# Attention queue three deep instead of two, VectorE's weight split one step later, and the second mixer's output products begun inside its last attention steps

## The reference, cut to what matters

```python
# second mixer: 16 heads of 64+32 (scores) and 64 (values)
q = (rms_norm(cq, q_norm_g) @ w_q_b).reshape(B, S, MLA_HEADS, MLA_NOPE + MLA_ROPE)
kv = (rms_norm(ckv, kv_norm_g) @ w_kv_b).reshape(B, S, MLA_HEADS, MLA_NOPE + MLA_V)
...
s = (einsum('bqhd,bkhd->bhqk', qn, k_nope) + einsum('bqhr,bkr->bhqk', qp, k_pe)) * scale
s = where(key_chunk[None, :] <= q_chunk[:, None], s, -inf)
o = einsum('bhqk,bkhd->bqhd', softmax(s, axis=-1), v)
h = o.reshape(B, S, MLA_MIX) @ w_out                       # "mout": 256x1024 @ 1024x1024
x = layer_norm(DN_ALPHA * x + h, ln_g[i, 0], ln_b[i, 0])   # "n2"
x = layer_norm(DN_ALPHA * x + swiglu_ffn(x, w_gate_up, w_down), ...)   # "gu", "down"
...
# last block: 8 + 8 heads of 64 with a bias, 8 of them with a sink in the softmax
y = concatenate([out_a, out_b], axis=-1) @ w_out            # "out2"
```

## Time and profile before

| what | value |
|---|---|
| median of 3 runs | 1254.49 us (1254.19 to 1254.67) |
| the profiled execution | 1250.47 us, of which the span of the trace is 1248.7 us |
| PE busy | 1135.4 us (91%) |
| DVE busy | 741.6 us (59%) |
| ACT busy | 519.6 us (42%) |
| chain that ended last | PE 81%, DVE 11%, ACT 4%, issue 3%, DMA 1% |
| granted TensorE clock, mean | 0.932 of full speed |

### The profile page before, as it was taken

How to read it: one execution, slowest core, us unless ns; L and a number is a source line. 1 busy time by engine, 2 the same in 40 slices (tenths; PEclk the granted TensorE clock), 3 DMA queues, 4 the chain that set the end, 5 groups by cost and what they waited for, 6 DMA issues and landing times.

```text
span 1248.7 us, 17256 instructions
## 1 busy us (share of the span) xinstructions
PE 1135.4 (91%) x7196; PEld 1000.8 (80%) x7196; DVE 741.6 (59%) x1046; ACT 519.6 (42%) x710; POOL 120.8 (10%) x115
## 2 busy tenths in 40 slices
PE   5989799997799999987988799999879996999997
PEld 5788699895699998766766699998668765999885
DVE  3485585447666666557665676666554536666433
ACT  3443322124344443234664354343355545565331
POOL 0005163220300000030000300000000000000000
PEclk9899899858799999987999799999979987999999
DMA  9345000004398678532692488678434212565640
GB/s 281 98 131 189 1 2 1 1 9 161 124 307 264 217 241 286 180 121 77 168 222 84 143 296 270 227 241 288 154 123 147 87 50 67 170 189 182 203 168 34
DMA packets 112270, 193.68 MB, mean 155 GB/s; under 512 B 4514, under 2 KB 84913, under 8 KB 112066
## 3 DMA queue, kind: packets, MB, share of 16 engines
q1 hardware_dynamic: 108530, 179.65, 43.3%
q0 software_dynamic: 3248, 11.83, 4.1%
q10 hardware_dynamic: 416, 1.11, 0.2%
HBM read 188.38 MB, written 4.19 MB: 154 GB/s over the span
## 4 chain that ended last, share of the span: by engine, by line
PE 81%; DVE 11%; ACT 4%; issue 3%; DMA 1%; POOL 0%; ACTq 0%; DVEq 0%
PE ps L406 22%; PE ps L407 21%; PE ps L408 21%; PE ps L1098 2%; PE ps L1851 2%; PE ps L1109 2%; PE ps L1116 1%; DVE XL L539 1%; PE ps L1335 1%; PE ps L1844 1%; DVE ARR L390 1%; PE ps L1866 1%; DVE AR L1071 1%; DVE STAT L556 1%; ACT ARR L379 1%
## 5 line engine op out<-in xcount | busy, mean ns | idle before, releaser
L390 DVE TENSOR_TENSOR ARR<-ring,ARR 128x2048 fp32r<-128x2048 f32 (+1 forms) x147 | 329.5, 2246 | 239.5 <-ACT ARR L379 239.4
L406 PE MATMUL ps<-XH,ARR 128*128 128x256 f32 x1232 | 354.8, 288 | 17.9 <-DVE XL L539 11.4
L379 ACT ACTIVATE ARR<-ring 128x2048 fp32r<-128x2048 f32 (+1 forms) x147 | 274.7, 1875 | 220.5 <-PE ps L408 167.6
L407 PE MATMUL ps<-XL,ARR 128*128 128x256 f32 x1232 | 351.3, 285 | 0.0
L408 PE MATMUL ps<-XH,ARR 128*128 128x256 f32 x1232 | 351.1, 285 | 0.0
L406 PEld LDWEIGHTS ps<-XH,ARR 128*128 128x128 f32 x1232 | 237.8, 193 | 24.3 <-issue 17.9
L407 PEld LDWEIGHTS ps<-XL,ARR 128*128 128x128 f32 x1232 | 237.9, 193 | 0.0
L408 PEld LDWEIGHTS ps<-XH,ARR 128*128 128x128 f32 x1232 | 237.6, 193 | 0.0
L406 PE MATMUL ps<-ARR 128*128 128x512 f32 x420 | 171.8, 409 | 9.0 <-DVE ARR L491 5.8
L407 PE MATMUL ps<-ARR 128*128 128x512 f32 x420 | 168.3, 401 | 0.0
L408 PE MATMUL ps<-ARR 128*128 128x512 f32 x420 | 168.3, 401 | 0.0
(11 more groups left out here) (335 smaller groups left out, 1338.9 us busy)
## 6 DMA issues: line engine op xcount, KB each, us to landing
ring<-in_ffn_w_gate_up_dram SPq DMA_DIRECT2D x44, 1024.0 KB, 5.6
ring<-in_w_dram SPq DMA_DIRECT2D x32, 1024.0 KB, 5.2
ring<-in_w_ada_dram SPq DMA_DIRECT2D x24, 1024.0 KB, 5.4
ring<-in_ffn_w_down_dram SPq DMA_DIRECT2D x22, 1024.0 KB, 5.0
ring<-in_even_w_in_dram SPq DMA_DIRECT2D x13, 1024.0 KB, 6.2
ring<-in_w_in_dram SPq DMA_DIRECT2D x9, 1024.0 KB, 5.3
ring<-in_mla_w_q_b_dram SPq DMA_DIRECT2D x6, 768.0 KB, 4.7
ring<-in_even_w_out_dram SPq DMA_DIRECT2D x4, 1024.0 KB, 4.9
```

Source lines behind the costliest of these rows:

```text
L379: e.activation(split(i)[0], raw(i), ACT.Copy).then_inc(*up("hi", ("hi", i)))
L390: e.tensor_tensor(lo, raw(i), hi.bitcast(F32), ALU.subtract).then_inc(*up("lo", ("lo", i), ("raw free", i)))
L406: e.matmul(out, lhs[0], rhs[0], start=first, stop=False)
L407: e.matmul(out, lhs[0], rhs[1], start=False, stop=False)
```

## The change

Three things change.

1. `LAG = 3` takes the place of 2 in both attentions: in step i TensorE transposes and multiplies head i-3, and ScalarE moves head i-3. The loops have one step more. VectorE still scales head i-1 in step i. A group leaves in step 4g+7 instead of 4g+6.
2. In the swa attention VectorE splits a piece in the step after the one in which ScalarE splits it. The output products that stood behind the loop are regrouped by one call for the additional step.
3. In the mla attention the first half of mout (pieces 0 and 2, both token halves) runs beside steps 15 to 18, two `pe_mout` calls in each, and `pe_mout_rest` runs the other half behind the loop. ScalarE splits mout's third piece beside step 12 and the fourth beside step 17, VectorE beside steps 13 and 18. `split_rest` for "mout" is gone on both engines. The scores and turned weights of the last steps keep to banks 2 and 0 so that mout can have 4, 5, 1 and 3.

```diff
+        LAG = 3
+
         def pe_attend(e, A, along=None):
             if A.heads:
                 pe_turn_head(e, 0)
-            for i in range(18):
+            for i in range(16 + LAG):
                 if A.heads:
                     pe_turn_head(e, i + 1)
-                if 0 <= i - 2 < 16:
-                    h = i - 2
+                if 0 <= i - LAG < 16:
+                    h = i - LAG
...
-            return {4 * g + 6: g for g in range(4)}.get(i)
+            return {4 * g + 4 + LAG: g for g in range(4)}.get(i)
...
-            lambda i: i % 2, lambda i: 2 + i % 2, heads=True)
+            lambda i: i % 2 if i < 15 else 0, lambda i: 2 + i % 2 if i < 15 else 2, heads=True)
+        MOUT_BANK = {(0, 0): 4, (0, 1): 5, (1, 0): 1, (1, 1): 3}
+
+        def pe_mout(e, k0, t, j):
+            use, w = ("mout", t, j), place_of["mout", k0]
+            if k0 == 0:
+                bank(e, use, MOUT_BANK[t, j])
+            if (t, j) == (0, 0):
+                e.wait_ge(*at(("lo", w)))
+                e.wait_ge(*at(("mla", "att", k0 // 2)))
+            for c in range(2):
+                k = mm3(e, ps(use), cut(XT, ALL, k0 + c, slice(t * P, t * P + P)),
+                        cut(split(w), ALL, c, slice(512 * j, 512 * j + 512)), k0 + c == 0, k0 + c == 7)
...
+        def pe_beside_mla(e, i):
+            if i >= 15:
+                for j in range(2):
+                    pe_mout(e, 2 * ((i - 15) // 2), (i - 15) % 2, j)
+
+        def act_beside_mla(e, i, late):
+            if late and i in (8, 10, 12):
+                act_split(e, place_of["mout", i - 8])
+            elif late and i == 17:
+                act_split(e, place_of["mout", 6])
+
+        def dve_beside_mla(e, i):
+            if i in (9, 11, 13):
+                dve_split(e, place_of["mout", i - 9])
+            elif i == 18:
+                dve_split(e, place_of["mout", 6])
+
+        def pe_mout_rest(e):
+            for k0 in (4, 6):
+                for t in range(2):
+                    for j in range(2):
+                        pe_mout(e, k0, t, j)
...
-            else:
+            elif i == 17:
                 for j in range(2):
                     for c in range(2):
                         pe_out2(e, 4, 0, j, c)
+            else:
+                for c in range(2):
+                    pe_out2(e, 4, 1, 0, c)
...
         def dve_beside_heads(e, i):
-            if i in SPLITS_2:
-                dve_split(e, place_of[SPLITS_2[i]])
+            if i - 1 in SPLITS_2:
+                dve_split(e, place_of[SPLITS_2[i - 1]])
...
-            pe_attend(e, MLA)
-            pe_rows(e, "mout", 8, 1024, XT, lambda c: ("mla", "att", c))
+            pe_attend(e, MLA, pe_beside_mla)
+            pe_mout_rest(e)
...
-            act_attend(e, MLA)
-            split_rest(act_split, e, "mout", 8, 2)
+            act_attend(e, MLA, act_beside_mla)
...
-            dve_attend(e, MLA)
-            split_rest(dve_split, e, "mout", 8, 2)
+            dve_attend(e, MLA, dve_beside_mla)
```

More of the change, by code:

```diff
@@ L1877, in act_attend @@
                 turn_head_out(e, 0, e.activation(QK[0][0:96, :], ps(("hd", 0))[0:96, :], ACT.Copy))
-            for i in range(19):
+            for i in range(17 + LAG):
                 if along:
@@ L1960, in program @@
             lambda h: [("hd", h)], lambda h: [], PR_MLA, PX_MLA, ST_MLA, None, ["odd"], XT,
-            lambda i: i % 2, lambda i: 2 + i % 2, heads=True)
+            lambda i: i % 2 if i < 15 else 0, lambda i: 2 + i % 2 if i < 15 else 2, heads=True)
[10 more added lines that the diff above has]
+                        cut(split(w), ALL, c, slice(512 * j, 512 * j + 512)), k0 + c == 0, k0 + c == 7)
+            here = [("full", use)] if k0 == 6 else []
+            if (t, j) == (1, 1):
+                here.append(("used", w))
+            if here:
+                k.then_inc(*up("products", *here))
+        def pe_beside_mla(e, i):
[17 more added lines that the diff above has]
+                        pe_mout(e, k0, t, j)
         BIAS = place(13320, 16, 256)
@@ L2124, in pe_beside_heads @@
                         pe_out2(e, 4, 0, j, c)
+            else:
+                for c in range(2):
+                    pe_out2(e, 4, 1, 0, c)
         def pe_out2_rest(e):
-            for j in range(2):
-                for c in range(2):
-                    pe_out2(e, 4, 1, j, c)
+            for c in range(2):
+                pe_out2(e, 4, 1, 1, c)
             for t in range(2):
```

## The result

The changed kernel takes 1247.01 us (median of 4 runs, 1246.06 to 1248.63) against 1254.34 us (4 runs, 1252.64 to 1254.67): ratio 0.9946, interval 0.9928 to 0.9963, so it is faster by 7.3 us (by the means of the same runs, which the ratio compares, 6.8). The profiled execution took 1247.66 us, with a span of 1245.7 us and a mean clock of 0.931.

What follows compares the result with a forecast made beforehand. TensorE, busy for 91% of the span, was taken to bound the kernel, gaining time only where it waits or runs slow. -10.6 - 2.6 + 8.5 = -4.7 us on the median 1254.5 gives 1249.8 us, range 1245.8 to 1255.4.

Steps and rivals of the forecast that it cites:

- the forecast's own bounds: Whole kernel: the ends of the three terms' bounds, combined in part, give 1247 to 1252.5 us.
- the rival in which ScalarE does not bind: mla attention: TensorE's own 2.40 us per step binds, some 3.5 us more gained, 1246.3 us; chance 0.08.
- the clock did fall in mla: mla attention: rival that ScalarE's step 12 split brings the clock down, costing 3.3 us, 1253.1 us; chance 0.25.
- Part 1: swa attention: deeper queue and later split remove two waits and their slow clock, 10.6 us gained, bounds 9.5 to 11.
- my slack: swa attention: everything stays hidden with at least 0.4 us in hand, at the move of head 7 or 11.
- Part 2: mla attention and mout: ScalarE sets steps, 5.23 us a pair; 2.6 us gained, bounds 1.0 to 4.5.
- the likelier case: mla attention: the forecast's case, the clock stays up behind the wait of 2.3 to 2.4 us; chance 0.45.
- The wait of 2.32 us: Earlier trace, at 288.07: a wait that did not bring the clock down, against falls behind 2.43 us.
- the tail: mla attention from head 15's scores on: 5.9 us of work against 6.32 us before, 0.4 us gained.
- Part 3: Feed-forward start: first gate piece no longer split ahead, TensorE waits 13 us, 8.5 us lost, bounds 6.7 to 9.6.
- a swa wait stays, or both: swa attention: one wait with slow clock survives, 1255.1 us, chance 0.09; both survive, 1260.4 us, chance 0.06.
- The swings of the clock in the mla loop: mla loop: small idles halve the clock in half of twelve steps, 14 us more, 1264 us; chance 0.02.

Runs made afterwards that it cites:

- the kernel with the mla queue alone: Queue three deep in the mla attention only, against the kernel before, mout still behind the loop: 1252.23 us, ratio 1.0002.
- The experiment that puts the two lines back: Changed kernel with the second feed-forward's first gate piece again split on ScalarE and VectorE right behind the mla attention: 1239.68 us, ratio 0.9893.
- the kernel with the late piece: Changed kernel with the gate piece split ahead and mout's third piece split in steps 16 and 17 instead of 12 and 13: 1236.31 us, ratio 0.9874.
- the swa part alone: Kernel before with only the swa attention's edits (queue three deep, VectorE's splits one step later, out2 regrouped): 1244.06 us, ratio 0.9924.

## Why the prediction was right, and where its terms were off

**Shift and sum.** Predicted -4.7, measured -7.3 by the medians (-6.8 by the means); 1247.0 lies within the range, at the lower end of the forecast's own bounds. The mechanism of all three terms is in the traces. The closeness of the sum is in part luck: two of the terms were off, by +1.3 and -0.75 us, and a fourth of -0.6 us was missing. Nor does the time tell the cases apart: it is nearest to that of the rival in which ScalarE does not bind (1246.3), which did not happen, while the clock did fall in mla, for which the price was 1253.1. The terms, each against its own stage:

**Part 1 (-10.6): right.** Both waits and both slow stretches are gone, nothing is late in their place: -10.89 us between the two profiles. The deeper queue by itself did leave a delay, the 0.64 us at the bank of the scores, so it is the later split that kept my slack whole. The size is softer than it looked: in the kernel with the mla queue alone the swa stage, with the same two waits of 2.43 us, took 94.67 instead of 96.38 us, since its first slow stretch was shorter. The term is then 9.2, below my bound of 9.5.

**Part 2 (-2.6): the mechanism right, the likelier case wrong.** Pairs of steps take 5.24 us (predicted 5.23), and 5.78 where a group leaves (5.71). The wait for the move of head 10 was 2.26 us (2.3 to 2.4). Without a fall of the clock the stage is 63.74 us, 2.4 under the 66.1 of the kernels before, close to the forecast's 2.6. But the clock fell in the profiled run and in two of the three others with this wait: the case to which I gave 0.25. The wait of 2.32 us that spoke for the other side was a weak witness: behind it TensorE worked only 0.66 us before its next wait, of 4.44 us, and in that the clock fell (window 288.73 to 290.80 at 1.00, 290.90 to 293.10 at 0.50). What that case had wrong is its price. I took the slow stretch of 6.7 us from the earlier trace rows; here it was 3.4 us, so that it cost 1.4 to 1.7 us and not 3.3, and the term is -1.3. In the tail -0.4 was predicted and -0.93 measured: the moves are hidden by mout as I had it, and the switching between kinds of matmul costs what I had charged (some 0.85 us by the start times, 0.8 predicted). Too large were the slots of the attention's own matmuls, for which I took lengths where the next kind begins before the last has ended: head 15's scores hold TensorE for 0.47 us (665.82 to 666.29) and not 0.82, and each of three sets of transposes for 0.30 and not 0.36.

The weak step was the placing of the split. I had costed it (1.90 us, and a wait at the edge of a fall) but not asked what would be left to gain without it. Of the 3.3 us that the third piece costs in step 12 (1.6 where the clock does not fall), all could be had by splitting it in step 16, where TensorE has mout to do.

**Part 3 (+8.5): right in kind, 0.75 too large.** TensorE started the piece 23.78 us behind the residual's first operation (713.49 - 689.71; predicted 713.0 - 689.29 = 23.71), with the clock low. From there the clock was low for 5.1 us (to 718.6) and not 6.7, which is 0.8 us of cost: +7.75 measured. The 6.7 us had no ground here: I had counted them from a wait that brings the clock down, and here it had been down since 698.2, as it had been in the kernel before from 697.1 to 710.6, which I had not read. The experiment that puts the two lines back finds 7.3.

**Not in the sum:** the banks, -0.6.

**The rivals.** That ScalarE does not bind falls with the waits on L1898 at a rhythm of 5.24. That a swa wait stays, or both, falls with the first window. The swings of the clock in the mla loop: TensorE idles 0.46 to 1.49 us in every second step, and the windows 626 to 658 of the changed kernel and 624 to 660 of the kernel with the late piece have a clock of 1.00. The rule of the Trainium skill on frequent small idles (TensorE: Matmul & The Clock Gate, section A second HAM failure mode: psum-queue depth-cycling) describes a swing that no run here shows at idles of this size and spacing.

**What the sum does not explain.** The terms as measured between the two profiles, with the banks, come to -5.5; if each stage is compared over all kernels that share it (66.2 against 64.9, 221.2 against 227.8, 33.1 against 32.5, 95.5 against 85.5), to -5.3. The medians say -7.3 and the means -6.8, with an interval of -9.0 to -4.6. Part of what lies between can be the sample of the kernel before: its four runs here have a median of 1254.34 us, the 18, 13 and 9 runs taken with the experiments 1253.20, 1252.81 and 1252.92, against which the changed kernel's 1247.01 is 5.8 to 6.2 us. All of it lies within the interval, and I have no further cause for it.

## What to carry to other kernels

Read what a helper that is deleted did besides its name: here it split the next stage's first weight, and two lines give back 7.3 us, about as much as the whole change brought. A deeper queue pays when the work that it leaves for the tail is covered; alone it moved the waits from the loop to behind it. When a wait must be placed, put it where the waiting engine has other work, and above all keep TensorE's waits short: in these traces the clock fell in some executions behind waits of 1.75 to 2.3 us, in all four cases behind one of 2.43 us in swa, and stayed up through a loop with waits of 0.46 to 1.49 us. Two edits, each of which alone shortened two waits of 2.4 us to 0.6, brought 8.9 and 9.8 us by the stage, 6.9 and 6.4 by the medians.

## What the runs showed of the hardware

**A wait near 2.3 us may or may not bring the clock down,** with the same instructions, and a shorter one can do it too. These are the windows from 616 to 622 us in the kernel before and in the one with the swa part alone, which are the same code up to there (length, PE busy, granted clock, DMA share, GB/s); the waits ahead are 1.77 and 1.79 us:

```profile
616.00:618.00 2.00, 2.00 (x11) 1.00 1.02 108
618.00:620.00 2.00, 2.00 (x10) 1.00 1.00 106
620.00:622.00 2.00, 1.49 (x10) 1.00 0.98 104
```
```profile
616.00:618.00 2.00, 0.98 (x3) 0.82 0.66 78
618.00:620.00 2.00, 2.00 (x7) 0.50 0.93 99
620.00:622.00 2.00, 2.00 (x9) 0.83 1.02 108
```

In the second the clock falls for some 3.4 us. All 13 profiles have this wait, of 1.74 to 1.79 us; in six the clock fell behind it (at 1.75 to 1.79 us), in seven it did not (1.74 to 1.79). Such falls are part of the run-to-run spread: head 0's scores begin at 626.1 to 629.1 us in the six and at 622.5 to 627.3 in the seven, after code that is the same, while a stage that runs at 1.00 throughout repeats to 0.02 us (swa, 85.47 to 85.49 in nine profiles of seven kernels). So a stage of the trace can show a tenth of a microsecond where medians of whole runs cannot show two.

**The slow stretch has no fixed length.** Behind the same wait of 2.43 us in swa it was 6.7 us in the kernel before and some 3.4 in this one (mla queue alone; wait ahead of 1000.74, PE):

```profile
1001.00:1002.00 1.00, 1.00 (x7) 1.00 1.04 367
1002.00:1003.00 1.00, 1.00 (x3) 0.50 1.09 389
1003.00:1004.00 1.00, 1.00 (x4) 0.50 0.38 117
1004.00:1005.00 1.00, 1.00 (x4) 0.50 0.00 0
1005.00:1006.00 1.00, 1.00 (x7) 0.79 0.00 0
1006.00:1007.00 1.00, 1.00 (x8) 1.00 0.00 0
```

Behind the 2.26 us in mla it was 3.4 us. The 5.1 us behind the feed-forward's wait of 13.4 us are the end of a stretch that had begun before that wait. By the costs here (1.4 to 1.7 us for the stretch of 3.4 us, and an estimated 3.3 for one of 6.7 us at half the rate) a term that rests on one slow stretch of one execution should carry a range of 1.5 to 3.5 us.
